# Sparse attention: one ScalarE copy takes the transposed blocks of both heads of a pair out of two neighbouring PSUM banks

## The reference, cut to what matters

```
s_c = q . kc + bias(distance);  p_c = masked_softmax(s_c);  o_c = p_c . vc      # 31 compressed keys
s_s = q . k_sel + bias;         p_s = masked_softmax(s_s);  o_s = p_s . v_sel   # selected blocks of 64 keys
s_w = q . kw + bias;            p_w = masked_softmax(s_w);  o_w = p_w . vw      # window of 512 keys
o = gate0 * o_c + gate1 * o_s + gate2 * o_w
```

## Time and profile before

| what | value |
|---|---|
| median of 3 runs | 2639.44 us (2635.38 to 2646.66) |
| the profiled execution | 2635.17 us, with a span of 2633.5 us |
| TensorE busy | 2476.2 us, 94% of the span |
| ScalarE busy | 967.7 us, 37% |
| VectorE busy | 1338.2 us, 51% |
| mean granted TensorE clock | 0.971 |

### The profile page before, as it was taken

One profiled execution on the slowest core, in us unless ns is written; L12 is line 12 of the kernel. 1 busy time (PEld: TensorE's weight loads), 2 busy tenths in 40 slices (PEclk: granted clock), 3 DMA queues, 4 the chain that ended last, 5 costly groups with the idle time before them and its releaser, 6 DMA issues.

```text
span 2633.5 us, 32260 instructions
## 1 busy us (share of the span) xinstructions
PE 2476.2 (94%) x12324; PEld 1999.1 (76%) x12324; DVE 1338.2 (51%) x2056; ACT 967.7 (37%) x1470; POOL 149.4 (6%) x132
## 2 busy tenths in 40 slices
PE   7999999989899999999999999998898878999996
PEld 6888876779778888867877788887776657788885
DVE  4444346575454443347655666633254773566633
ACT  4222237441442232253324333423234663433322
POOL 2000010022010000030001000001010001000001
PEclk9999999999999999999999999999898889999998
DMA  4333222210123333221112233323652102333321
GB/s 139 97 96 96 96 73 81 72 49 17 56 80 96 96 89 103 93 63 55 49 35 86 80 96 96 95 96 84 149 140 82 38 15 64 88 96 96 101 91 48
DMA packets 310548, 215.30 MB, mean 82 GB/s; under 512 B 40842, under 2 KB 294301, under 8 KB 310441
## 3 DMA queue, kind: packets, MB, share of 16 engines
q1 hardware_dynamic: 307176, 199.88, 26.3%
q0 software_dynamic: 3264, 13.94, 1.6%
HBM read 211.65 MB, written 8.44 MB: 84 GB/s over the span
## 4 chain that ended last, share of the span: by engine, by line
PE 82%; DVE 7%; ACT 6%; issue 2%; POOL 1%; DMA 1%; POOLq 0%; ACTq 0%; DVEq 0%
PE bank L504 16%; PE bank L506 16%; PE bank L505 16%; PE bank L644 6%; PE bank L643 6%; PE bank L642 6%; PE bank L817 2%; POOL rstd L763 1%; ACT arena L2567 1%; DVE arena L2493 1%; PE bank L2009 1%; ACT wH L381 1%; DVE wL L409 1%; PE bank L2400 1%; PE bank L1493 1%
## 5 line engine op out<-in xcount | busy, mean ns | idle before, releaser
L504 PE MATMUL bank<-xH,wH 128*128 128x512 f32 (+2 forms) x1992 | 798.4, 401 | 52.9 <-DVE xL L716 17.6
L506 PE MATMUL bank<-xH,wL 128*128 128x512 f32 (+2 forms) x1992 | 785.2, 394 | 0.0
L505 PE MATMUL bank<-xL,wH 128*128 128x512 f32 (+2 forms) x1992 | 784.8, 394 | 0.0
L409 DVE TENSOR_TENSOR wL<-raw,wH 128x1024 fp32r<-128x1024 f32 (+2 forms) x365 | 449.7, 1233 | 562.8 <-ACT wH L381 562.4
L381 ACT ACTIVATE wH<-raw 128x1024 fp32r<-128x1024 f32 (+2 forms) x365 | 379.0, 1039 | 828.0 <-PE bank L506 404.8
L504 PEld LDWEIGHTS bank<-xH,wH 128*128 128x128 f32 (+2 forms) x1992 | 374.0, 188 | 157.9 <-issue 36.7
L505 PEld LDWEIGHTS bank<-xL,wH 128*128 128x128 f32 (+2 forms) x1992 | 374.7, 188 | 86.4 <-issue 4.1
L506 PEld LDWEIGHTS bank<-xH,wL 128*128 128x128 f32 (+2 forms) x1992 | 373.9, 188 | 86.6
L644 PE MATMUL bank<-g_hi,wL 128*128 128x512 f32 x704 | 280.9, 399 | 0.0
L642 PE MATMUL bank<-g_hi,wH 128*128 128x512 f32 x704 | 276.3, 393 | 1.2 <-DVE wL L409 1.2
L643 PE MATMUL bank<-g_lo,wH 128*128 128x512 f32 x704 | 277.4, 394 | 0.0
(11 more groups left out here) (327 smaller groups left out, 2709.1 us busy)
## 6 DMA issues: line engine op xcount, KB each, us to landing
raw<-in_ffn_w_in SPq DMA_DIRECT2D x88, 512.0 KB, 3.8
raw<-in_w_up SPq DMA_DIRECT2D x88, 512.0 KB, 3.8
raw<-in_ffn_w_out SPq DMA_DIRECT2D x44, 512.0 KB, 3.5
raw<-in_w_down SPq DMA_DIRECT2D x44, 512.0 KB, 3.5
raw<-in_w_mix_in SPq DMA_DIRECT2D x28, 512.0 KB, 3.8
raw<-in_gla_w_in SPq DMA_DIRECT2D x16, 384.0 KB, 3.2
raw<-in_w_kv_shared SPq DMA_DIRECT2D x12, 512.0 KB, 6.5
rel_wide<-rel_rows POOLq DMA_DIRECT2D x12, 512.0 KB, 12.1
```

The costliest lines, as they stand in the source:

```text
L409: nc.vector.tensor_tensor(wL[:, h, 0:n], raw[:, k, 0:n], wH[:, h, 0:n].bitcast(F32), ALU.subtract)\
L504: pe.matmul(o, wh, xa, start=a, stop=False)
L505: pe.matmul(o, wh, xb, start=False, stop=False)
L506: last = pe.matmul(o, wl, xa, start=False, stop=z)
```

## The change

The eight PSUM banks are declared as one tensor, and `bank[b]` becomes a view of it, which leaves every other use of a bank as it was. `turned_act` then issues one activation for each part in place of two. Its input is a view of banks 5 and 6 (head, column), its output the matching two pieces of `ptb`. It waits until both heads are transposed, and adds 2 to `n_pts`. TensorE's program isn't edited. Its waits `2*j-1+u` are still in it, but the count now goes up by two at a time.

```diff
-        bank = [ctx.enter_context(nc.psum_tensor(f"bank{b}", [P, S], F32)) for b in range(8)]
+        banks = ctx.enter_context(nc.psum_tensor("banks", [P, 8 * S], F32))
+        bank = [banks[:, b * S:(b + 1) * S] for b in range(8)]
...
-            for u in range(2):
-                act.wait_ge(sem("n_turned"), 2 * j + u + 1)
-                r, n = (NCMP, S) if t is None else (P, P * (t + 1))
-                at = 1024 * u + 512 * br
-                nc.scalar.activation(ptb[q % 2][0:r, at:at + n], bank[5 + u][0:r, 0:n], ACT.Copy).then_inc(sem("n_pts"), 1)
+            act.wait_ge(sem("n_turned"), 2 * j + 2)
+            r, n = (NCMP, S) if t is None else (P, P * (t + 1))
+            to = ptb[q % 2].rearrange("p (u c) -> p u c", u=2)[0:r, :, 512 * br:512 * br + n]
+            turned = banks[0:r, 5 * S:7 * S].rearrange("p (u c) -> p u c", u=2)[:, :, 0:n]
+            nc.scalar.activation(to, turned, ACT.Copy).then_inc(sem("n_pts"), 2)
```

## The result

| | before | changed |
|---|---|---|
| median of 20 runs | 2637.8 us (2630.05 to 2652.04) | 2655.82 us (2648.41 to 2659.12) |
| ratio to before | | 1.0056 (95% interval 1.0043 to 1.0070) |
| profiled execution | 2635.17 us | 2658.72 us |

The changed kernel is slower by 0.56% of 2637.8, 14.8 us (11 to 18). The forecast was 8 us and its range held the time, but the likeliest case, no change that can be told, isn't what came. The result lies just beyond the 0.5%, on the side that had 0.24, and its interval, 0.43 to 0.70%, reaches to both sides of that line. The ratio goes with the means of the 20 times, which differ by 14.9 us; the medians differ by 18.

What follows compares the result with a forecast made beforehand. A closed chain through TensorE, ScalarE and VectorE in the attention stage was taken as the bound. Lost overlap of 1.36 us for each of six pairs gave 8.2 us, so 2647 us against the median, range 2637 to 2660.

Steps and rivals of the forecast that it cites:

- the side that had 0.24: Whole kernel: chance given to a measurably slower result, above 2652.6 us; faster had 0.02, same 0.74.
- the joint copies called covered: Attention stage, copies of (t1,0), (t0,0) and (t0,1): their delays were claimed to be hidden by other waits.
- The six terms of the cycle: Delays before turn(t2,0) 0.22, turn(t2,1) 0.08, turn(t3,0) 0.45, turn(t3,1) 0, turn(C) 0.24, exp(t1) 0.37 us.
- "I take the same 1.36 for" the last pair: Last attention pair, with no next pair's scores between its transposes: delay estimated at 1.36 us, like the five cycles.
- "I count none more and none less, and take it into the range": TensorE's clock in the attention stage: the number of slow, half-clock stretches was taken as unchanged.
- case 1: Attention stage: overlap lost as summed, clock unchanged, +8 us (+4 to +12), no change that can be told; chance 0.62.
- rival 2: Attention stage: clock falls once more for each pair, 9 us on top, 17 in all, 2656 us, slower; chance 0.20.
- My full-clock cycle of 22.5 us: Attention cycle from 2117.45: 24.0 us with one slow stretch, so claimed to take 22.5 at full clock.
- Rivals 3, 4 and 5: ScalarE bound, 2.7 us faster, 0.06; two-bank read costs two instructions, +13 us, 0.07; slow stretches mostly go, -4 us, 0.05.
- one of the signs of being wrong: Profile after: others were copies well over 1.02 us, or a one-slow-stretch cycle not about 25.4 us.

## Why the prediction was off

**What held.** The mechanism of the waits. The added waits on the chain lengthened the cycles, rest moved off it shortened them, and the joint copies called covered changed nothing. The chain holds for the order of the kernel before only: with rest moved it goes through VectorE's queue, and the same joint copies cost 0.2 us a cycle there. The prices of the joint copy (1.02, 0.81, 0.59 us) hold within 0.01. The six terms of the cycle add up to 1.40 us where 1.36 was forecast, each within 0.04. (Two readings in the working were off by a little and move nothing: the wait given as 1.58 us is 1.56 in the earlier trace rows, and the line gives 1.03 us where 1.02 was taken.) "I take the same 1.36 for" the last pair held as well, in the first profile, where the tail grew by 1.4 us (17.63 against 16.22). 6 x 1.4 = 8.4 us. ScalarE wasn't the bound, and its 3.6 us less busy time were worth nothing.

**What failed.** The step is "I count none more and none less, and take it into the range". The half-clock stretches are not a background that stays: they change with the waits, as filling one wait in each cycle showed. Counted in steps of 0.25 us, the stage of the kernel before has 8 of them with 34 us in all, the changed one has 9 with 38 us in its first profile and 12 with 65 us in each of the other two. With two buffers the five cycles had 23.8 us of half clock, in the two profiles of the changed kernel with a fast compression stage 48.0. Of the 15.1 us that the stage grew there, 8.4 are the six terms, and most of the other 6.7 is the clock, worked out as what remains: 136.10 - 124.92 = 11.2 us in the five cycles, of which 7.0 are waits, leaves 4.2, and the last pair's 3.6 (19.80 against 16.22) less 1.4 leaves 2.2. In the execution with a slow compression stage the stage grew by 9.2 us alone, with 27.0 us of half clock. So the same kernel pays 9 or 15 us for the change in the stage. Three profiles don't show what decides which. That the range held 2655.8 us is partly luck: case 1 had 4 to 12 us and 2643 to 2652, and it was rival 2 that carried the range to 2660.

**The price of a slow stretch.** The prediction priced every one at 1.5 us, from scores(t3). There it isn't worth that on the chain. A cycle with one such stretch took 23.99 us before and one without takes 23.42, so it costs 0.6 us, since max(t3) waits for scale(t1) on VectorE in the meantime. At the turns of t2 a stretch costs 1.5 us (24.94 - 23.42) and the longer one of the locked cycle 2.1. My full-clock cycle of 22.5 us was too short by 0.9 for the same reason, and the slow stretches cost 1.6 us a cycle before (124.92 - 5 x 23.42 = 7.8 for five), not 2.5.

**The rivals.** The result lies between the forecast and rival 2, and its mechanism is that rival's: at the wait before turn(t2,0) the clock falls. With 12 stretches for 8 the stage had four more, not six, and six of the 12 were longer ones, where two of the 8 had been. That the count changes by more than two was one of the signs of being wrong, and it came in two of the three profiles. A cycle with one stretch, at the turns, went from 24.94 to 26.45 us, by 1.5, about as the waits say. Rivals 3, 4 and 5 are out: no gain from fewer instructions, no cost of the two-bank read, no recovery of the clock. By the waits alone the case "no change that can be told" would have held. Among the waits, I foresaw those of TensorE at over 22 us and found 20.5, and those of ScalarE near 30 or more and found 44.3.

**What stays open.** 12 of the 20 first times of the changed kernel are above 2653, where the executions with the slow compression stage seem to lie, against 6 of 20 in the upper group before; one of the six taken again is. The products lie ahead of the edit in the same execution, and the declaration alone was not slower. Whether the change has a part in how often they fall to half clock wasn't settled. If the two groups are these two kinds of execution, the change costs 13.4 us within the lower group (2636.6 to 2649.9) and 10.7 within the upper (2647.1 to 2657.8), and what the 14.8 has beyond that comes from the shares of the groups. Why the cycle locks at 27.33 us rather than elsewhere isn't known either.

## What to carry to other kernels

Fusing two instructions that serve two buffers makes one buffer of them: before doing it, look whether the producer and the consumer use the overlap, by asking when the first of the two starts and who is released by its end. Here 3.6 us of busy time on an engine with slack were paid for with 8.4 us of waits. The price belongs to the chain of the moment: with one step of VectorE moved, the same fusion cost 0.2 instead of 1.4 us a cycle at full clock. On a chain where TensorE waits once or twice in each cycle, price the clock as a function of the waits, at the place where the slow stretch falls, and not as a constant. A cycle that repeats at a length above its full-clock sum is a sign of it.

## What the runs showed of the hardware

One ScalarE copy can read two neighbouring PSUM banks at full rate: 1024 columns took 1.024 us, where two copies of 512 took 1.06 to 1.09. Idle TensorE time cost twice here: 12 transposes of the identity, with no use, in a wait of 2 us in five of the six pairs made the kernel before 0.39% faster, and its five cycles had 9.9 instead of 23.8 us at half clock. In the locked cycle of the changed kernel TensorE had waited 1.7 us ahead of the turns that ran at half clock. And a stretch of 256 small matrix products with TensorE busy all the time ran at 1.00 clock in 14.3 us in some executions, and mostly at 0.50, in 24.7 us, in others of kernels that have the same instructions up to there.
